# Expert passes with 68 widths in steps of four columns instead of 20 in steps of sixteen

## The reference

```python
def _moe_swiglu(h, w_router, w_gate, w_up, w_down):
    tok = h.reshape(-1, D)                                  # 1024 tokens
    logits = (tok @ w_router).astype(jnp.float32)
    top_val, top_idx = lax.top_k(logits, TOP_K)             # 2 of 8
    weights = jax.nn.softmax(top_val, axis=-1)
    ...
    group_sizes = jnp.bincount(flat_e, length=N_EXPERTS)
    g = lax.ragged_dot(xs, w_gate, group_sizes)             # 1024 -> 3584
    u = lax.ragged_dot(xs, w_up, group_sizes)
    y = lax.ragged_dot(jax.nn.silu(g) * u, w_down, group_sizes)
    ...
```

## Time and profile before

| what | value |
|---|---|
| median of 3 runs | 3846.16 us (3839.22 to 3846.71) |
| the profiled execution's own time | 3847.34 us |
| its span | 3845.3 us |
| PE busy | 3615.9 us, 94% of the span |
| DVE, ACT busy | 60%, 43% |
| mean granted clock of TensorE | 0.969 |
| expert phase, first matmul to end | 1482 to 3845 us |

### The profile page before, as it was taken

How to read it: one execution, slowest core, us unless ns; L and a number is a source line. 1 busy time by engine, 2 the same in 40 slices (tenths; PEclk the granted TensorE clock), 3 DMA queues, 4 the chain that set the end, 5 groups by cost and what they waited for, 6 DMA issues and landing times. The chain is left out here.

```text
span 3845.3 us, 61241 instructions
## 1 busy us (share of the span) xinstructions
PE 3615.9 (94%) x22550; PEld 3312.0 (86%) x22551; DVE 2289.6 (60%) x2986; ACT 1659.4 (43%) x1924; POOL 423.3 (11%) x364
## 2 busy tenths in 40 slices
PE   7989998999999985999999999999999899999997
PEld 4986577888888754899999999988899898999997
DVE  3557643445445546866555555567555698665677
ACT  4226533233232254654443343346533455444444
POOL 0007400000000001010000010001100100100673
PEclk8999999999999997999999999999999999999998
DMA  6513235333522226954453443459444475543764
GB/s 225 219 46 131 109 110 189 98 98 98 153 98 92 79 95 208 343 183 168 143 173 131 131 149 131 150 179 341 158 143 152 146 241 175 190 152 127 234 220 147
DMA packets 409780, 610.88 MB, mean 159 GB/s; under 512 B 23126, under 2 KB 337110, under 8 KB 409608
## 3 DMA queue, kind: packets, MB, share of 16 engines
q1 hardware_dynamic: 386152, 542.02, 41.8%
q0 software_dynamic: 23168, 65.68, 5.5%
q10 hardware_dynamic: 288, 1.05, 0.1%
HBM read 586.80 MB, written 41.98 MB: 164 GB/s over the span
## 5 line engine op out<-in xcount | busy, mean ns | idle before, releaser
L2593 DVE TENSOR_TENSOR moe_gu_lo<-moe_raw_gu_lo,moe_gu_hi 128x2048 fp32r<-128x2048 f32 x254 | 587.2, 2312 | 114.6 <-ACT moe_gu_hi L2412 114.1
L2412 ACT ACTIVATE moe_gu_hi<-moe_raw_gu_lo 128x2048 fp32r<-128x2048 f32 x254 | 486.0, 1914 | 321.3 <-DMA moe_raw_gu_lo<-in_moe_w_gate 248.9
L2247 PE MATMUL moe_g<-moe_x,moe_gu_hi 128*128 128x336 f32 (+4 forms) x1344 | 414.7, 309 | 24.2 <-issue 15.2
L2649 DVE SCALAR_TENSOR_TENSOR moe_y_t<-moe_y,moe_cols,moe_y_t 128x288 f32<-128x288 f32 (+4 forms) x728 | 371.6, 535 | 104.9 <-PE moe_y L2249 104.3
L2248 PE MATMUL moe_g<-moe_x,moe_gu_hi 128*128 128x336 f32 (+4 forms) x1344 | 414.9, 309 | 0.0
L2249 PE MATMUL moe_g<-moe_x,moe_gu_lo 128*128 128x336 f32 (+4 forms) x1344 | 413.7, 308 | 0.7 <-issue 0.7
L2247 PE MATMUL moe_y<-moe_h,moe_d_hi 128*128 128x336 f32 (+4 forms) x1344 | 411.7, 306 | 0.0
L2248 PE MATMUL moe_u<-moe_x,moe_gu_hi 128*128 128x336 f32 (+4 forms) x1344 | 410.9, 306 | 0.0
L2248 PE MATMUL moe_y<-moe_h,moe_d_hi 128*128 128x336 f32 (+4 forms) x1344 | 410.7, 306 | 0.0
L2247 PE MATMUL moe_u<-moe_x,moe_gu_hi 128*128 128x336 f32 (+4 forms) x1344 | 409.5, 305 | 0.0
L2249 PE MATMUL moe_u<-moe_x,moe_gu_lo 128*128 128x336 f32 (+4 forms) x1344 | 409.4, 305 | 0.0
(11 more groups left out here) (421 smaller groups left out, 8485.3 us busy)
## 6 DMA issues: line engine op xcount, KB each, us to landing
moe_raw_gu_lo<-in_moe_w_gate SPq DMA_DIRECT2D x127, 1024.0 KB
moe_raw_gu_lo<-in_moe_w_up SPq DMA_DIRECT2D x127, 1024.0 KB
moe_raw_d_lo<-in_moe_w_down SPq DMA_DIRECT2D x126, 1024.0 KB
ffn_raw_d_lo<-in_ffn_w_down SPq DMA_DIRECT2D x22, 1024.0 KB, 4.9
proj_w_mod<-in_w_ada POOLq DMA_DIRECT2D x10, 2048.0 KB, 10.1
att_w_mod<-in_w_ada SPq DMA_DIRECT2D x10, 2048.0 KB, 7.8
ffn_first_raw<-in_ffn_w_gate SPq DMA_DIRECT2D x11, 1024.0 KB, 5.5
ffn_first_raw<-in_ffn_w_up SPq DMA_DIRECT2D x11, 1024.0 KB, 7.9
```

What stands on the lines that cost most here:

```text
L2247: pe.matmul(bank[:, 0:width], wh, moving[:, 0, 0:width], start=start, stop=False)
L2412: act.activation(hi[par][:, :, :], raw[par][:, :, :], ACT.Copy).then_inc(rounded, 1)
L2593: dve.tensor_tensor(lo[par][:, :, :], raw[par][:, :, :], hi[par][:, :, :].bitcast(F), ALU.subtract).then_inc(split, 1)
L2649: dve.scalar_tensor_tensor(y_t[:, db, 0:cols], y_ps[db % 4][:, 0:cols], gate, y_t[:, db, 0:cols], ALU.mult, ALU.add).then_inc(y_added, 1)
```

## The change

`ROUND` becomes 4, and with it `WIDTHS` has 3 + 65 = 68 entries. The starts of the table's comparison are cut to the first four widths. Above 256 the number of the width is found by scaling the tokens over 256 by 1/4 and rounding to a whole number, by adding and subtracting 1.5 x 2^23 in fp32. The half of an expert of two passes is found the same way, and the table `half_of`, its load and its comparison go.

```diff
-ROUND = 16
+ROUND = 4
...
+        LOW = WIDTHS.index(256) + 1
...
-            sp.dma_start(half_of[:, :], dram["half_starts"].partition_broadcast(P)).then_inc(ld, 16)
...
             dve.tensor_scalar(small["over"][:, :], chose, float(TOKENS), None, ALU.is_gt)
-            dve.tensor_tensor(halves[:, :, :], chose.unsqueeze(2)..., half_of[:, :].unsqueeze(1)..., ALU.is_gt)
             link(dve.tensor_scalar(small["any"][:, :], chose, 0.0, None, ALU.is_gt))
-            dve.reduce_sum(small["half"][:, :], halves[:, :, :], AX.X)
+            dve.tensor_scalar(small["half"][:, :], chose, 0.5 / ROUND, (2 * ROUND - 1) / (4 * ROUND), ALU.mult, ALU.add)
             link(dve.tensor_tensor(small["passes"][:, :], small["over"][:, :], small["any"][:, :], ALU.add))
+            link(dve.tensor_scalar(small["half"][:, :], small["half"][:, :], 1.5 * 2 ** 23, None, ALU.add))
+            link(dve.tensor_scalar(small["half"][:, :], small["half"][:, :], -1.5 * 2 ** 23, None, ALU.add))
...
-            link(dve.tensor_tensor(above[:, :, :], ...[P, M, len(WIDTHS)]), ..., ALU.is_gt))
-            link(dve.reduce_sum(table_f[:, 1, :], above[:, :, :], AX.X))
+            dve.tensor_tensor(above[:, :, :], ...[P, M, LOW]), ..., ALU.is_gt)
+            link(dve.tensor_scalar(steps[:, :], count[:, :], -float(WIDTHS[LOW - 1]), 0.0, ALU.add, ALU.max))
+            dve.reduce_sum(table_f[:, 1, :], above[:, :, :], AX.X)
+            link(dve.tensor_scalar(steps[:, :], steps[:, :], 1.0 / ROUND, (ROUND - 1) / (2 * ROUND), ALU.mult, ALU.add))
+            link(dve.tensor_scalar(steps[:, :], steps[:, :], 1.5 * 2 ** 23, None, ALU.add))
+            link(dve.tensor_scalar(steps[:, :], steps[:, :], -1.5 * 2 ** 23, None, ALU.add))
+            link(dve.tensor_tensor(table_f[:, 1, :], table_f[:, 1, :], steps[:, :], ALU.add))
```

More of the change, by code:

```diff
@@ L1597, in routing_phase @@
         M = MAX_PASSES_PAD
+        LOW = WIDTHS.index(256) + 1
         started, ended, here, part, counts = (sb(n, [P, M, E]) for n in ("started", "ended", "here", "part", "counts"))
-        count, above, table_f = sb("count", [P, M]), sb("above", [P, M, len(WIDTHS)]), sb("table_f", [P, 2, M])
-        width_of = sb("width_of", [P, len(WIDTHS)])
-        half_of, halves = sb("half_of", [P, TOKENS // ROUND]), sb("halves", [P, E, TOKENS // ROUND])
+        count, above, table_f = sb("count", [P, M]), sb("above", [P, M, LOW]), sb("table_f", [P, 2, M])
+        width_of, steps = sb("width_of", [P, len(WIDTHS)]), sb("steps", [P, M])
         spare_starts = sb("spare_starts", [P, LISTED_TILES])
@@ L1667, in _ @@
             m.then_inc(logit_mm, 1)
-            pe.wait_ge(ld, 16 * 10)
+            pe.wait_ge(ld, 16 * 9)
             pe.wait_ge(either_ok, 1)
@@ L1706, in _ @@
             dve.wait_ge(logit_mm, 1)
-            dve.wait_ge(ld, 16 * 10)
+            dve.wait_ge(ld, 16 * 9)
             dve.tensor_copy(token_f[:, :], keep["tokens"][:, :])
@@ L1738, in _ @@
             dve.tensor_scalar(small["over"][:, :], chose, float(TOKENS), None, ALU.is_gt)
-            dve.tensor_tensor(halves[:, :, :], chose.unsqueeze(2).to_broadcast([P, E, TOKENS // ROUND]),
-                              half_of[:, :].unsqueeze(1).to_broadcast([P, E, TOKENS // ROUND]), ALU.is_gt)
             link(dve.tensor_scalar(small["any"][:, :], chose, 0.0, None, ALU.is_gt))
-            dve.reduce_sum(small["half"][:, :], halves[:, :, :], AX.X)
+            dve.tensor_scalar(small["half"][:, :], chose, 0.5 / ROUND, (2 * ROUND - 1) / (4 * ROUND), ALU.mult, ALU.add)
             link(dve.tensor_tensor(small["passes"][:, :], small["over"][:, :], small["any"][:, :], ALU.add))
+            link(dve.tensor_scalar(small["half"][:, :], small["half"][:, :], 1.5 * 2 ** 23, None, ALU.add))
+            link(dve.tensor_scalar(small["half"][:, :], small["half"][:, :], -1.5 * 2 ** 23, None, ALU.add))
             link(dve.tensor_scalar(small["gap2"][:, :], small["half"][:, :], float(-ROUND), float(TOKENS), ALU.mult, ALU.add))
@@ L1795, in _ @@
             dve.reduce_sum(table_f[:, 0, :], part[:, :, :], AX.X)
-            link(dve.tensor_tensor(above[:, :, :], count[:, :].unsqueeze(2).to_broadcast([P, M, len(WIDTHS)]),
-                                   width_of[:, :].unsqueeze(1).to_broadcast([P, M, len(WIDTHS)]), ALU.is_gt))
-            link(dve.reduce_sum(table_f[:, 1, :], above[:, :, :], AX.X))
+            dve.tensor_tensor(above[:, :, :], count[:, :].unsqueeze(2).to_broadcast([P, M, LOW]),
+                              width_of[:, 0:LOW].unsqueeze(1).to_broadcast([P, M, LOW]), ALU.is_gt)
+            link(dve.tensor_scalar(steps[:, :], count[:, :], -float(WIDTHS[LOW - 1]), 0.0, ALU.add, ALU.max))
[4 more added lines that the diff above has]
+            link(dve.tensor_tensor(table_f[:, 1, :], table_f[:, 1, :], steps[:, :], ALU.add))
             link(dve.tensor_copy(table_f[:, 0, M - 1:M], ends[:, E - 1:E]))
```

## The result

| | median of runs, us | lowest to highest | profiled execution, us | its span, us |
|---|---|---|---|---|
| before | 3846.5 (9 runs) | 3838.5 to 3852.6 | 3847.3 | 3845.3 |
| after | 3875.0 (9 runs) | 3854.4 to 3879.2 | 3876.9 | 3874.9 |

The change made the kernel slower: ratio 1.0071, 95% interval 1.006 to 1.0082, 28.5 us in the medians and 29.6 us in the profiled executions. The forecast was 3835 us, with a range that ended at 3850.

A forecast was written before the change was run, and what follows sets the result against it. PE, busy 94% of the span, was taken to bound the kernel by its own pace inside wide passes. Terms -17.8 + 1.8 + 1.5 + 3 - 0.3 = -11.8 us on 3847.3 gave 3835.5, a median of about 3835; range 3821 to 3850.

The forecast's parts named there:

- On PE I take 0, since the loop's jump over 608 costs 0.21: PE's jump from `tail` to `head`, now over 103 instructions: no added cost; upper bound 29 us over eight borders.
- The tree costs a fetch on PE at each border: Rival: `tail` and `head` in different blocks, eight more jumps of 3.3 to 3.9 us, 3864 us; chance 0.08.
- L2046 was never one in nine: Argument against the rival of a fetch per border: PE's jump from `tail` to `head` was never far in nine times.
- The widths: PE's matmuls in five changed passes: intervals interpolated between measured widths, 17.8 us less in sum.
- the sign of a wrong main term: Check on the five changed passes together: main term wrong if they shorten by less than 12 or more than 24 us.
- The new widths carry the larger extra: Rival on PE's matmul intervals: gain only 0.2 us against costs of 6.0, 3852 us; chance 0.16.
- The tree's 18 branches more: Choice of the program: 62 branches instead of 44, 2.9 us by kind, 1.8 us counted.
- The jump to program 2: Jump into the narrow pass's program (width 144), now 74 instructions later: near or far, 0 to 3.3 us, 1.5 taken.
- The +3 for DVE and ACT at the end of the loop: Far jumps to `head` on DVE and ACT, uncovered at the loop's end: 0 to 9 us, 3 taken once.
- Routing: Computing half and width: the half 0.3 us less on the path, the width about 1.4 instead of 1.04 us, covered.
- followed by more matmuls at half clock: After each far jump on PE, in the rival of a fetch per border, more matmuls at half clock; no separate size.
- Steps of 16: Rival: PE takes columns in steps of 16, so new widths run as multiples of 16, 3868 us; chance 0.06.

The follow-up runs named there:

- experiment 1: The changed kernel with the block `tail` moved right ahead of `head` on all three engines: 3846.4 us, ratio to before 1.0007.
- experiment 6: The kernel before, old widths and short tree, with `tail` placed behind program 1, on PE 628 instructions behind `head` instead of 29: 3880.2 us, ratio 1.0087.
- experiment 8: The changed kernel with 128, 65 or 194 never-run instructions ahead of `head`, distances kept: 3855.0, 3863.2 and 3858.1 us.
- experiments 4 and 5: Small kernels without the model, timing PE's matmuls per width, then from eight starts per width (no total given); also the changed kernel rerun word for word: 3868.0 us.
- experiment 3: The changed kernel with a table of 20 programs, including the five new widths, so a tree as short as before: 3845.4 us, ratio 1.0002.
- experiment 7: The changed kernel with `tail` ahead of `head` on PE alone, ACT and DVE keeping it behind the tree: 3849.6 us, ratio 1.0013.

## Why the prediction was wrong

**The step that failed** is "On PE I take 0, since the loop's jump over 608 costs 0.21" for the jump from `tail` to `head`. Its seven far ones last 32.7 us in the trace; without them the median is 28.5 us lower (experiment 1), and made far in the kernel before it costs 34.9 (experiment 6). The bound stated was 29. The inference was from the wrong witness. The loop of 608 instructions had just run through its code; `head` had not run for a whole pass. The block of `tail` was there (the leaving jump took 0.2 to 0.4 us), presumably by its hint, but no run leaves the hint out. Experiment 6 makes the comparison fair: 628 instructions back to a `head` that has not run for a pass is far. "L2046 was never one in nine" said that `tail` and `head` shared a block while 29 apart, and nothing about 103 apart. I had priced this as the rival "The tree costs a fetch on PE at each border" with 3864 us, and gave it 0.08. It deserved five times as much: a border that falls at random in 256 instructions hits a stretch of 31 in one of eight cases and one of 103 in four of ten, an estimate by the block size that experiment 8 supports. The Trainium skill's rule (Runtime: NRT & Kernel Launch, "Instruction fetch mechanics"), that a taken branch out of the blocks held waits for a fetch, spoke for it, and the trace of after agrees with 3.4 to 5.0 us a time. At six of the seven borders that is longer than the jump into a program, 3.3 to 3.9.

**The widths**, the largest term, were mis-sized too. Predicted were 157.3, 155.3, 149.5, 136.3 and 130.4 ns, measured 157.8, 155.0, 148.9, 139.9 and 131.5: the sum is 4.1 ns less than before, 8.3 us instead of 17.8. From first to last matmul the five passes shorten by 6.3 us, under the 12 that the prediction named as the sign of a wrong main term; the rest goes to slower starts, that of pass 340 above all (granted clock 0.58 in its first 10 us, against 0.83 for the 336 before). 300 alone missed by 3.6 ns, 7.3 us, and lay above its own bound of 139.5. The sum is within the bounds of 0.2 and 34, but the choice of the middle rested on a smooth curve that does not exist (experiments 4 and 5), and the 8.3 us are partly luck of the draw: with the paces of experiment 3 the same widths give 2.4. So the rival "The new widths carry the larger extra" (0.2 us) was on this term about as near as the forecast.

**The other terms.** The sum of the terms gives 3834.3 for the median, which the prediction rounds to "about 3835". The tree's 18 branches more were counted right (48 + 9 + 5 = 62) and 1.8 us can't be seen in the times. The jump to program 2 went far, 3.55 us, but border and narrow pass together grew by only 0.5 us with two far jumps in them, since PE waits for DVE later in that pass: after, the longest such wait is 5.3 us, before it was 7.2. So 1.5 was too much. The +3 for DVE and ACT at the end of the loop holds about: their jump to `head` is far in experiment 7 and gone in experiment 1, and DVE's wait differs by 3.5 us, the time from PE's last matmul to the end by 4.4. Routing: from the start of `over` to that of the first `gap` it was 1.14 us and is 0.97, 0.2 less where I had said 0.3; from `above` to the copy of `ends` it was 1.04 us and is 1.30, under cover, since DVE then still waits 1.98 us for PE's list. That each far jump is "followed by more matmuls at half clock" does not show: in the first 10 us of the five changed passes the granted clock was 0.68, 0.83, 0.85, 1.00 and 0.62 before and is 0.75, 0.58, 0.82, 0.85 and 0.80 now, higher at two and lower at three, and the first two matmuls of pass 344 start 0.45 us apart, as before. (The 0.45 us were a poor witness: they are nearly three times the pace. The next ones, 0.29 to 0.30 us apart before and 0.29 after, are the half clock.)

**Steps of 16** are excluded: 340 ran at 155.0 and 328 at 148.9 ns, not at 161 and 153. The half and the number of the widths came out as the table says.

## What to carry to other kernels

A block that closes a loop belongs next to the block that opens it, or ahead of it so that it falls in: what lies between them decides whether the way back is a fetch, and where a border of code blocks falls decides whether a small shift of code costs 3 to 5 us at most turns (experiment 8). When a table of programs or a tree grows, look for every branch whose source and target move apart, and take the near time only from a branch whose target has lately run. Before columns are saved in steps finer than those measured, measure the pace of the very widths, more than once.

## What the runs showed of the hardware that was not expected

- The same matmul stream runs at one of several fixed paces and keeps it, in the passes of 284 until PE waits: 284 columns at 131.1 or 133.3 ns, 300 at 136.7, 137.8 or 139.9 ns, 328 at 148.9, 150.0 or 151.1, 340 at 153.4 or 155.0, 344 at 153.4 or 157.8. Most paces repeat with a period of three or six matmuls (146, 149, 152 ns for 328 in after), while 328 in experiment 3 takes 149 to 151 ns each time. What draws the pace was not found.
- 304 columns are never slower than 300 in these traces by more than 1.2 ns, and up to 2.2 ns faster.
- A far jump on PE takes mostly 3.3 to 4.1 us into a program (1.9 to 4.7 at the ends) and 3.2 to 5.3 back to `head`, and on ACT and DVE it does not show in the branch's own time (0.05 us) but in the gap behind it (2.3 to 5.0 us).
